# Copying the v table into whole rows inside DRAM, gathering it with one DMA a batch, and adding the gathered sums to the residual

## What is computed

```python
q = (x_tok @ w_q).reshape(t, PEER_HEADS, 2, D_HALF)      # 8 heads
...
experts = e1 * N_KEYS + e2            # 16 of 128*128 experts for each token and head
g = jax.nn.softmax(top_s, axis=-1)
u_sel = peer_u[experts]
act = jax.nn.gelu(jnp.einsum('td,thkd->thk', x_tok, u_sel), approximate=False)
coef = act * g
v_sel = peer_v[experts]               # peer_v: (16384, 2048) float32, 134 MB
return jnp.einsum('thk,thkd->td', coef, v_sel)
...
x = layer_norm(DEEPNORM_ALPHA * x + f, ln2_g, ln2_b)     # f: the result above
```

## Time and profile before

| what | value |
|---|---|
| median of three runs | 1907.87 us |
| profiled execution, its own time | 1898.23 us |
| span of its trace | 1896.4 us |
| PE busy | 1779.9 us (94%) |
| DVE busy | 1363.7 us (72%) |
| ACT busy | 855.4 us (45%) |
| POOL busy | 670.2 us (35%) |
| moved by DMA | 433.27 MB, mean 228 GB/s |
| mean granted TensorE clock | 0.978 |

### The profile page before, as it was taken

The page is one execution under the profiler, slowest core; times in us unless marked ns, Lnnn a source line. Parts: engine busy times, 40 slices in busy tenths (PEclk is TensorE's granted clock), DMA queues, the critical chain, the costliest instruction groups (busy, mean ns, idle before and its releaser), DMA issues.

```text
span 1896.4 us, 33625 instructions
## 1 busy us (share of the span) xinstructions
PE 1779.9 (94%) x12090; PEld 1627.9 (86%) x12090; DVE 1363.7 (72%) x1903; ACT 855.4 (45%) x1212; POOL 670.2 (35%) x425
## 2 busy tenths in 40 slices
PE   8999999899999999999999999969695999999996
PEld 8999978899999999999999999847574777777875
DVE  7998985699937777777764445557483787888866
ACT  5544444444444444444444444524242445444443
POOL 0000024678961000000000000677786787777201
PEclk9999999999999999999999999989897999999999
DMA  7665556555566555555556565769695999999863
GB/s 277 225 211 191 184 167 215 189 173 175 170 209 229 183 182 186 183 181 188 181 189 194 191 193 191 230 201 332 220 346 187 383 350 369 332 348 366 293 210 114
DMA packets 137934, 433.27 MB, mean 228 GB/s; under 512 B 34304, under 2 KB 34432, under 8 KB 136320
## 3 DMA queue, kind: packets, MB, share of 16 engines
q1 hardware_dynamic: 97440, 359.97, 55.9%
q0 software_dynamic: 22528, 67.16, 9.7%
q10 hardware_dynamic: 17888, 5.26, 1.2%
HBM read 423.83 MB, written 8.39 MB: 228 GB/s over the span
## 4 chain that ended last, share of the span: by engine, by line
PE 71%; POOL 11%; issue 8%; DMA 5%; DVE 4%; ACT 2%; SPq 0%; DVEq 0%; POOLq 0%; ACTq 0%
PE psum L1409 18%; PE psum L1410 18%; PE psum L1411 18%; POOL rows L532 5%; DMA raw<-in_v_w_dram 4%; POOL sp_act L538 4%; PE psum L1576 3%; PE psum L1578 2%; PE psum L1577 2%; PE psum L1580 2%; PE psum L1581 2%; DVE w_lo L815 2%; PE psum L1543 1%; PE psum L1453 1%; PE psum L1455 1%
## 5 line engine op out<-in xcount | busy, mean ns | idle before, releaser
L575 ACT ACTIVATE w_hi<-raw 128x1024 fp32r<-128x1024 f32 x652 | 691.2, 1061 | 936.4 <-PE psum L1411 484.3
L815 DVE TENSOR_TENSOR w_lo<-raw,w_hi 128x1024 fp32r<-128x1024 f32 x568 | 688.6, 1224 | 310.3 <-ACT w_hi L575 303.3
L1409 PE MATMUL psum<-xt_hi,w_hi 128*128 128x256 f32 x2944 | 827.1, 281 | 15.5 <-DVE xt_lo L829 9.3
L1410 PE MATMUL psum<-xt_lo,w_hi 128*128 128x256 f32 x2944 | 824.6, 280 | 0.0
L1411 PE MATMUL psum<-xt_hi,w_lo 128*128 128x256 f32 x2944 | 823.7, 280 | 0.0
L1409 PEld LDWEIGHTS psum<-xt_hi,w_hi 128*128 128x128 f32 x2944 | 555.2, 189 | 17.4 <-issue 11.5
L1411 PEld LDWEIGHTS psum<-xt_hi,w_lo 128*128 128x128 f32 x2944 | 555.1, 189 | 0.0
L1410 PEld LDWEIGHTS psum<-xt_lo,w_hi 128*128 128x128 f32 x2944 | 555.0, 189 | 0.0
L532 POOL DMA_INDIRECT rows<-in_v_w_dram,sp_idx x256 | 364.4, 1423 | 148.1 <-issue 101.6
L538 POOL DMA_INDIRECT sp_act<-act_spill,sp_idx x64 | 78.6, 1228 | 626.2 <-DMA act_spill<-stage 585.5
L1576 PE MATMUL psum<-w_hi,c_hi 128*128 128x512 f32 x504 | 204.3, 405 | 78.9 <-DVE w_lo L815 76.7
(11 more groups left out here) (193 smaller groups left out, 1165.1 us busy)
## 6 DMA issues: line engine op xcount, KB each, us to landing
raw<-in_u_w_dram SPq DMA_DIRECT2D x256, 512.0 KB
raw<-in_v_w_dram SPq DMA_DIRECT2D x256, 512.0 KB
raw<-in_w_in_dram SPq DMA_DIRECT2D x80, 512.0 KB
raw<-in_w_out_dram SPq DMA_DIRECT2D x32, 512.0 KB
raw<-in_w_q_dram SPq DMA_DIRECT2D x32, 512.0 KB
act_spill<-stage ACTq DMA_DIRECT2D x32, 128.0 KB, 2.3
rows<-in_v_w_dram,sp_idx POOLq DMA_INDIRECT x256
xt_raw<-in_x_t_dram SPq DMA_DIRECT2D x4, 512.0 KB, 7.5
```

The lines of the kernel that those rows point to most:

```text
L575: nc.scalar.activation(parts_of(slot_u)[0][:, :], raw[:, slot_u % RAW, :], ACT.Copy).then_inc(hi_done, 1)
L815: tt(lo_w[:, :], raw[:, slot_u % RAW, :], hi_w[:, :].bitcast(f32), ALU.subtract).then_inc(lo_done[slot_u % SPLIT], SPLIT)
L1409: mm(dst, hi_w[:, sl], xt_hi[:, kk, :], start=st, stop=False)
L1410: mm(dst, hi_w[:, sl], xt_lo[:, kk, :], start=False, stop=False)
```

## The change

Three things change.

First, `v_rows`, a new 134 MB tensor in DRAM, holds `peer_v` with each expert's 2048 columns in one piece. The kernel fills it itself with 256 DMAs from `v_w`, each 512 KB, from DRAM to DRAM, in pieces of 2 KB (L445 of the kernel after). They are issued on SP's queue between the loads of units 12 to 392: two for every three loads. POOL waits for all of them before its first gather.

Second, a pick's rows are fetched by one indirect DMA of 8 KB a partition in place of four of 2 KB. The index calculation shrinks. The activations after the first 16 are fetched one or two behind each row gather (`acts_issued`), not 16 in a row. The picks move to U_DOWN + 20 + 206*k//64.

Third, the sparse sums don't pass through the fold. One DMA moves the half on partitions 0 to 63 to partitions 64 to 127 (`half_in`), and DVE adds both halves, divided by ALPHA, to the residual (`add_picked`). The fold keeps two matmuls and one split, and stands earlier: chunks 0 and 1 one chunk after their end, chunk 2 and 3 within the last pass at its second and fourth unit, instead of its fourth and seventh.

```diff
+V_UNITS = 2 * NCH * GROUPS
+COPY0, COPY1 = 12, U_DOWN - 8
 def pick_unit(k):
-    return U_DOWN + 14 + (U_LAST - U_DOWN - 16) * k // PICKS
+    return U_DOWN + 20 + (U_LAST - U_DOWN - 18) * k // PICKS
+def acts_issued(k):
+    return min(PICKS, PICKS_IN + (4 * max(0, k - ROWS + 1) + 2) // 3)
...
-        v_rows = v_w.rearrange("u p (e c) -> (u p e) c", c=DCH)
+        v_rows = nc.dram_tensor("v_rows", [N_KEYS * N_KEYS, D], f32, kind="Internal").ap()
+        v_rows_of = v_rows.rearrange("(p g e) (j c) -> p g e j c", p=P, e=2, c=DCH)
...
+            def copy_unit(n):
+                g, j, h = n // (2 * NCH), n // 2 % NCH, n % 2
+                sp.dma_start(v_rows_of[:, 2 * g + h, :, j, :], v_w[n].rearrange("p (e c) -> p e c", c=DCH))\
+                    .then_inc(v_copied[n % 2], 16)
+            def copies_by(u):
+                return V_UNITS * min(max(u - COPY0, 0), COPY1 - COPY0) // (COPY1 - COPY0)
             def stream(src, base, first, end):
-                with sp.Fori(first // RAW, end // RAW) as i:
-                    for s in range(RAW):
-                        load(s, src[RAW * i + s], base + RAW * i + s)
+                for n in range(first, end):
+                    u = base + n
+                    load(n % RAW, src[n], u)
+                    for m in range(copies_by(u), copies_by(u + 1)):
+                        copy_unit(m)
...
-                for j in range(NCH):
-                    nc.gpsimd.indirect_dma_start(
-                        rows[k % ROWS][:, j * DCH:(j + 1) * DCH], None, v_rows,
-                        bass.IndirectOffsetOnAxis(sp_idx[:, 1 + j, k:k + 1], 0)).then_inc(rows_in[k % ROWS], 16)
+                nc.gpsimd.indirect_dma_start(
+                    rows[k % ROWS][:, :], None, v_rows,
+                    bass.IndirectOffsetOnAxis(sp_idx[:, 1, k:k + 1], 0)).then_inc(rows_in[k % ROWS], 16)
...
+            for done in v_copied:
+                pool.wait_ge(done, 16 * V_UNITS // 2)
             for k in range(2):
                 gather_rows(k)
...
-            for n in range(1, PICKS // PICKS_IN):
-                gather_acts(n)
-                for k in range(ROWS + 8 * (n - 1), ROWS + 8 * n):
-                    gather_rows(k)
+            for k in range(ROWS, PICKS):
                 gather_rows(k)
+                gather_acts(acts_issued(k - 1), acts_issued(k))
+            pool.wait_ge(picked_done, PICKS)
+            nc.gpsimd.dma_start(rows[2][P - SPARSE:P, :], picked[0:SPARSE, :]).then_inc(half_in, 16)
...
-                nc.scalar.activation(s_part[j % 2][0][:, :], picked[:, j * DCH:(j + 1) * DCH], ACT.Copy)\
-                    .then_inc(split_hi, 1)
...
+            def add_picked(n):
+                ...
+                stt(res[mine, TB - 1, :], part[mine, :], 1.0 / ALPHA, res[mine, TB - 1, :],
+                    ALU.mult, ALU.add).then_inc(res_added, 1)
...
-                mm(v_bank(j, 1), dense, y_part[j % 2][0][:, :], start=True, stop=False)
-                mm(v_bank(j, 1), dense, y_part[j % 2][1][:, :], start=False, stop=False)
-                mm(v_bank(j, 1), sparse, s_part[j % 2][0][:, :], start=False, stop=False)
-                mm(v_bank(j, 1), sparse, s_part[j % 2][1][:, :], start=False, stop=True).then_inc(folded, 1)
+                mm(v_bank(j, 1), fold[:, :], y_part[j % 2][0][:, :], start=True, stop=False)
+                mm(v_bank(j, 1), fold[:, :], y_part[j % 2][1][:, :], start=False, stop=True).then_inc(folded, 1)
...
-                            if (g, h) == (G_LAST + 1, 1):
-                                fold_chunk(2)
-                            if (g, h) == (G_LAST + 3, 0):
-                                fold_chunk(3)
+                            if (g, h) in ((G_LAST, 0), (G_LAST + 1, 0)):
+                                fold_chunk(2 + g - G_LAST)
```

More of the change, by code:

```diff
@@ L377, in build @@
         coef_done = sem("coef_done")
+        v_copied = [sem(f"v_copied{i}") for i in range(2)]
         rows_in = [sem(f"rows_in{i}") for i in range(ROWS)]
@@ L389, in build @@
         coef_at = {down_unit(g, 0): g + 1 for g in range(GROUPS - 1)}
-        split_at = {U_LAST + 2 * LAST * (j + 1) + 3: j for j in range(NCH - 2)}
-        split_at[U_LAST + 2 * LAST * (NCH - 1) + 5] = NCH - 2
+        split_at = {U_LAST + 2 * LAST * (j + 1) + (1 if j < NCH - 2 else 5): j for j in range(NCH - 1)}
         PER_HEAD = 2 * 11 + 2 + 12
@@ L1294, in split_low @@
             def split_low(j):
-                dve.wait_ge(split_hi, 2 * j + 2)
+                dve.wait_ge(split_hi, j + 1)
                 tt(y_part[j % 2][1][:, :], v_bank(j, 1), y_part[j % 2][0][:, :].bitcast(f32),
                    ALU.subtract).then_inc(split_lo, 1)
-                tt(s_part[j % 2][1][:, :], picked[:, j * DCH:(j + 1) * DCH], s_part[j % 2][0][:, :].bitcast(f32),
-                   ALU.subtract).then_inc(split_lo, 1)
+            def add_picked(n):
+                mine = slice(P - SPARSE, P)
+                if n == 0:
+                    dve.wait_ge(picked_done, PICKS)
+                    dve.wait_ge(res_in, 16)
+                    part = picked
+                else:
+                    dve.wait_ge(half_in, 16)
+                    dve.wait_ge(res_added, 1)
+                    part = rows[2]
+                stt(res[mine, TB - 1, :], part[mine, :], 1.0 / ALPHA, res[mine, TB - 1, :],
+                    ALU.mult, ALU.add).then_inc(res_added, 1)
             onehot1(0)
@@ L1343, in _ @@
                         pick(k)
-                if u in split_at and u < U_END - 2 * LAST:
+                if u in split_at:
                     split_low(split_at[u])
                 j, n = (u - U_LAST) // (2 * LAST), (u - U_LAST) % (2 * LAST)
-                if u >= U_LAST and 1 <= j < NCH - 1 and n < 2:
-                    dve.wait_ge(used, USED0 + U_LAST + 2 * LAST * j)
-                    if n == 0:
-                        dve.wait_ge(res_in, 16)
-                        added = add_down(0, j - 1)
-                    else:
-                        chunk_stats(0, j - 1, chain[0], x2_in)
-                if u >= U_LAST and j == 2 and n == 5:
-                    add_folded(0)
+                if u >= U_LAST:
+                    if j == 0 and n in (5, 7):
+                        add_picked((n - 5) // 2)
+                    if j and n == (2 if j < NCH - 1 else 6):
+                        dve.wait_ge(used, USED0 + U_LAST + 2 * LAST * j)
+                        dve.wait_ge(res_in, 16)
+                        chunk_stats(0, j - 1, add_down(0, j - 1), x2_in)
+                    if 0 < j < NCH - 1 and n == 4:
+                        add_folded(j - 1)
             def centre2(b, d):
```

56 lines of the change are left out of this document (18 added, 38 removed).

## The result

The changed kernel takes 1884.89 us (median of 4 runs, 1880.05 to 1892.89), the kernel before in the same series 1908.55 us. The ratio is 0.9875, with a 95% interval of 0.9825 to 0.9924: 24 us faster, where 64 were forecast. The kernel before was measured anew in each series (medians 1905.31 to 1908.98 us), and every ratio is taken within one series. The profiled execution takes 1880.05 us, its span 1878.2.

What follows compares the result with a forecast made beforehand. PE bounds the stages before the down stage, where it waits for DVE, late through POOL's gathers. From 1898.2 us: -57.0 - 6.2 + 5 + 0 - 5.7 = 1834.3, plus 9.6 carried over: 1844 us, range 1820 to 1990.

Steps and rivals of the forecast that it cites:

- the copy at 0: Stages before the down stage: 256 copies priced like loads, PE stays the bound, cost 0; high end +227 us.
- break-even points: Copied byte's cost in loaded ones at which cover ends, against 410 GB/s: 1.5 first stage, 1.8 up stage.
- rival 1: Units 12 to 392: copies make early stages DMA-bound, ACT waits for raw, +72 to +227 us; chance 0.36.
- The estimate by the page of the Trainium skill: Copies between HBM tensors at 214 to 186 GB/s would cost +45 to +135 us; the forecast took 0 instead.
- the three long pauses: Down stage: PE's waits of 17.91, 15.93 and 23.14 us for w_lo go, -57.0 us.
- the slow clock: Down stage: PE's slow start after each long pause goes too, 3 x 2.05, -6.2 us.
- the small ones: Down stage: PE's other 11 pauses, 0.8 to 3.2 us each, stay; their 20 us left as they are.
- the end: After the down stream: shorter, earlier fold and POOL free sooner, -5.7 us, of which 1.9 is PE.
- the +5: Down stage: loads of residual and norm weights fall into a full DMA stream, +5 us (0 to 10).
- The block of 16: Down stage: 16 activation gathers before picks 4, 12 and 20 hold POOL 24 us or more, making rows late.
- rivals 2 and 3: Down stage: DMA-bound, +32 us, 1876, chance 0.10; or DVE's picks wait for rows again, 1900 to 1930, chance 0.04.
- the carry of 9.6 us: Whole kernel: runs' median lies 9.6 us above the profiled execution; added to 1834.3 to give 1844 us.

Runs made afterwards that it cites:

- e1: No-layer kernel of back-to-back 512 KB DMAs: 24 loads 34.3 us, 24 copies as in the change 73.8, 24 loads mixed with 16 copies 74.0.
- near rows: Changed kernel with v_rows in another row order, so a copy's 2 KB pieces lie 16 KB apart: 1833.36 us, ratio 0.9634.
- the padded kernel: Changed kernel with 129 rows per first key in place of 128, so a copy's pieces lie 1 MiB + 8 KiB apart: 1834.27 us, ratio 0.9616.

## Why the prediction was wrong, point by point

**Wrong in one term: the copy at 0.** That term failed, and it is the one for which the text gave a range of 0 to +227. The reason for its low end was that the nearest rows read at 340 GB/s and write at 323. Both rows are true, and neither has the pattern of the copy: the 323 GB/s of the earlier trace rows is one write of 2 MB. The copy's pieces of 2 KB lie exactly 1 MiB apart, and at this pitch a copy costs 2.15 times a load when only copies run (1.2 times with 8 KiB more of pitch) or, mixed with loads, (74.0 - 34.3)/16 = 2.48 us to a load's 1.43, 1.7 times. The text's own break-even points are 1.5 in the first stage and 1.8 in the up stage, so 1.7 names the first stage as the late one, and there most of the loss arises. But it does not size the loss. Those points measure the room against 410 GB/s, which the trace had for 10 us only; against the sustained 361 they are 1.15 and 1.4. And with e1's prices a unit of the up stage would need 1.43 + 0.674 x 2.48 = 3.10 us of DMA against PE's 2.81, which over some 250 units is 70 us, where 18 arise between the transposes of x1 and the down stage. The windows are nearer: the mixture moved 293 GB/s in the first stage, where 340 were needed, and 300 in the up stage, where 311 were. For the first stage that gives 174 x (340/293 - 1) = 28 us (22.8 measured), for the up stage 27, still more than the 18. The mechanism was that of rival 1, with all its signs: ACT's 259 us of waits for `raw<-in_u_w_dram` and a down stage from 1233.5 us. Its price was set too high, 130 where 47.5 was measured, so the kernel still ended faster. The estimate by the page of the Trainium skill, +45 to +135, held it at its low end. That it hit so near is luck: the low end takes 214 GB/s, and the copies alone ran at 171, which by the same sum would be some 200 us. What the page had right was the direction, and I had set it aside for rows that did not show the pattern.

**Right: the three long pauses go.** They did, with the slow clock behind them (0.95 to 0.99), and the small ones stayed: 20 us left as they are, 17.9 measured. The down stage lost 62.0 us; the sum had -57.0, -6.2, +5 and 1.9 of PE at the end, -60.1. No run measures the +5 by itself.

**Right, but incomplete: why POOL was late.** The block of 16 was named as the cause. With the block left in place and one gather a pick, only 11 us are lost; with the block gone and four gathers, the kernel is 125 us slower, which stays unexplained in part. The blocks showed themselves in the profile because POOL had no room left at four gathers (6.9 us a pick and 48 x 1.53/60 = 1.2 for the activations, of 7.5), so it never made good what a block cost. So the pauses are not the block's alone. The reading that fits both runs is that the load took away the room and the block was the moment; it is argued, not shown by itself. And the 6.9 us are not POOL's own price: beside an idle DVE the four gathers need 5.0.

**Right: rivals 2 and 3 are out.** DMA share in the down stage is 0.86, and a gather of 8 KB a partition costs POOL 1.67 us, not 6.9. That POOL pays by the issue and not by bytes was right.

**Right: the end.** PE's last matmul, 3.9 us to POOL's start, one chunk: as written. 3.8 us behind the last matmul are measured; with the fold's 1.9, which is reckoned and not measured by itself, they give the 5.7.

**Wrong by 10 us, and hidden: the carry of 9.6 us.** The profiled execution of before was 9.6 us under its median, and I carried that over. Without the copy's price the kernels' medians are 1833 to 1835 us, not 1844. So the sum of 1834.3 without the carry is what those kernels took. The runs of before spread over 1900.59 to 1918.93 us in one series, those with near rows, in the same series, over 1833.15 to 1834.38. If the pauses' length differs between executions, what goes with a pause takes its spread along. That the pauses are the reason was not measured by itself, and the padded kernel's runs spread over 11 us again.

## What to carry to other kernels

Before you price a new transfer by a similar row, compare the pattern on both sides, the size of the pieces and the distance between them; where 128 pieces lie exactly 1 MiB apart, try a padding of one row first. Such a price has a threshold below which it costs nothing: work out the break-even factor from the stage's room at a rate that the trace sustains, and then measure the transfers in their mixture, since the prices of the parts alone came out too high here (83.4 us for 74.0). Where an engine is late after a block of work, ask whether it had any room to catch up before you blame the block, and whether the mean length of its instructions is its own or depends on a neighbour.

## What the runs showed that was not expected

- Copies within DRAM run at 305 to 308 GB/s on one core, 0.83 of a load's rate (367 to 370), in 4 KB pieces in order or in 2 KB pieces 1 MiB + 8 KiB apart.
- At exactly 1 MiB the same copies run at 217 GB/s (4 KB) or 171 (2 KB). At 512 KiB they run at 256, at 16 KB at 249, both with 2 KB pieces.
- Loads suffer only with 2 KB pieces: 249 GB/s at 1 MiB, 318 at 16 KB, 360 at 512 KiB; with 4 KB pieces 1 MiB apart, 368.
- Issuing the copies from a second engine's queue changed 74.0 us to 72.5.
- An indirect gather costs POOL 0.94 to 0.97 us when it begins beside an idle DVE, whether it fetches 8 KB a partition, 2 KB or 4 bytes: its price is per issue. The means of 1.67, 1.42 and 1.23 us (the earlier trace rows for the latter two) differ by how often DVE was running: beside it, the same issues took 1.70, 1.56 and 1.46.
